# A hybrid encoder in fp32 on one core: one weight block loaded into another buffer, one transposition and some vector steps in new places

## The chip, the cores and the metric

The kernel runs on one core of one Trainium2 chip. The metric is the device time of one execution in microseconds (us). Engines by the names of the profile: PE is TensorE, with PEld its weight loads; DVE is VectorE, ACT ScalarE, POOL GpSimd, and SP the queue of SyncE, which only issues transfers here.

## What is computed

Two layers over 512 tokens of width 1024. Each layer has a mixer (window attention beside a spatial gate) and an MLP of width 4096. The change touches only the start of the MLP and its weights, so the mixer stands here as one line.

```python
for l in range(DEPTH):
    x = x + mixer(rms_norm(x, norm_mix[l]))             # attention beside spatial gating
    h = rms_norm(x, norm_ffn[l])
    x = x + jnp.square(jax.nn.relu(h @ w_up[l])) @ w_down[l]
return rms_norm(x, norm_final)
```

## The kernel before

**Precision by parts.** Every weight block (128x1024, 512 KB) comes into a slot of `raw` (6 slots). ACT rounds it into `whi` (line 932, the high part), and DVE (line 1289; in the mixer and for the first four blocks of an MLP, POOL, line 535) writes what is left into `wlo`, the low part. Both have 5 slots and are used in the order of PE's groups. The other operand is split in the same way (`xhi`/`xlo`, `sxhi`/`sxlo`, `fhi`/`flo`). A product is three matmuls: high by low, high by high, low by high (lines 576 to 581).

**Seven products.** The MLP is done in four quarters of its width. In each, UP (h by w_up) and DOWN (the squared hidden values by w_down) are 2x2 block products by a scheme with seven block products M1 to M7 in place of eight; some factors are sums of blocks. UP runs M1, M2, M7, M6, M4, M5, M3, DOWN runs M1, M7, M6, M4, M5, M2, M3. Each product has two groups of weights (g = 0, 1). An up product is 48 matmuls of 256 columns, a down product 24 of 512. In the last quarter of a layer, `last_products` runs M2 and M3 by halves of the tokens: M2, M3, M2, M3, of 12 matmuls each, with the turns of the next norm between them.

**Where weights come from.** M1 (B11), M2 (B21), M3 and M7 (B22) are plain loads by SP (`load_block`). The weights of M7, M5 and M4 of DOWN are completed by a transfer that POOL issues and that adds a block onto the slot (`add_block`, line 548); those of M6, and M4 of UP, are summed on DVE (`sum_m6` line 1566, `sum_m4` line 1573). `PRODUCT_SLOT` says which pair of slots of `raw` a product has: M7, M6 and M4 share slots 2 and 3 one after another, M1 and M5 slots 0 and 1, M2 and M3 slots 4 and 5. A load waits until the low part of the slot's last block is made (`wait_low`). SP issues in the order of its program and stands at each wait.

**What PE waits for in DOWN.** M6, M4, M5 and M3 build on banks that DVE has just added to the residual `xt` (`add_product`, line 1586): M3 waits for the add of M5, M5 for the add of M6 (`ADDS_TO`). In DVE's order the add of M5 stands behind both low parts of M3.

**Start of the MLP.** The last of the four tiles of the norm is transposed on PE (`turn`, line 603) behind up product M1. From it `xs_make` and `xs_low` (lines 1503 to 1518) build four summed factors: S3 (for M7), S2 (M6), S5 (M5) and S4 (M3); ACT rounds them in `xs_high` (line 1137). `copy_sum` (line 1145) copies M1's, M7's and M6's banks, `up_sum` (line 1529) adds products to them, `hidden` (lines 1157, 1159) makes relu and square. Up product M4 may start when M7's banks are copied, M3 when M5 is summed. The order on each engine is that of its program; no scheduler moves anything.

Of the kernel before, what the change touches and what calls it, by code (L numbers as in the profile page):

```python
# [73 lines left out]
PRODUCT_SLOT = (0, 4, 4, 2, 0, 2, 2)  # L74
# [3 lines left out]
PHASE_LOADS = (1, 1, 1, 1, 2, 2)  # L78
# [29 lines left out]
def loads(l, slot):  # L108
    return l * (MIX_LOADS[slot] + 2 * QUARTERS * PHASE_LOADS[slot])
# [6 lines left out]
def block_loads(l, q, ph, r, g):  # L116

    slot = PRODUCT_SLOT[r] + g
    return loads(l, slot) + MIX_LOADS[slot] + (2 * q + ph) * PHASE_LOADS[slot] + (2 if r == M3 else 1)
# [9 lines left out]
def raw_slot(n):  # L129
    l, pos = divmod(n, PER_LAYER)  # L130
    if pos < MLP_POS:
        return mix_slot(pos)
    i, at = divmod(pos - MLP_POS, PER_PHASE)
    return PRODUCT_SLOT[SEQUENCE[i % 2][at // 2]] + at % 2

# [95 lines left out]
def build(nc, x, gains, weights, sinks, ws, bs, alibi, ident_in, out):  # L231
    with ExitStack() as ctx:
# [206 lines left out]
        def _(sp):  # L439
# [3 lines left out]
            def load_mix(l, pos):  # L443
                if pos >= 4:
                    wait_low(sp, nth(l, pos - 4))
                elif l:
                    wait_low(sp, nth(l - 1, group_pos(QUARTERS - 1, DOWN, M4 if pos < 2 else M5, pos % 2)))
                load(l * LAYER_ROWS + pos, mix_slot(pos))

            def load_block(l, q, ph, r, g):  # L450

                before = divmod(phase(l, q, ph) - 1 - l * 2 * QUARTERS, 2)
                if r == M3:
                    wait_low(sp, nth(l, group_pos(q, ph, M2, g)))
                    if ph == UP:
                        sp.wait_ge(weights_summed, summed_weights(l, q, UP, M4, g))
                elif q or ph:
                    wait_low(sp, nth(l, group_pos(*before, {M1: M5, M7: M4, M2: M3}[r], g)))
                elif r != M2:
                    wait_low(sp, nth(l, MLP_POS - 4 + PRODUCT_SLOT[r] + g))  # L460
                elif l:
                    wait_low(sp, nth(l - 1, group_pos(QUARTERS - 1, DOWN, M3, g)))
                load(block_row(l, q, ph, PRODUCT_BLOCK[r], g), PRODUCT_SLOT[r] + g)
# [33 lines left out]
            for l in range(DEPTH):  # L497
# [31 lines left out]
        def _(pool):  # L529
# [8 lines left out]
            def add_block(l, q, ph, r, g):  # L538

                slot = PRODUCT_SLOT[r] + g  # L540
# [29 lines left out]
        def _(pe):  # L570
# [167 lines left out]
            def up_product(l, q, r):  # L738
# [4 lines left out]
                for m in range(PAIRS):  # L743
                    h, part = divmod(m, 2)
# [90 lines left out]
            for l in range(DEPTH):  # L835
# [78 lines left out]
        def _(act):  # L914
# [66 lines left out]
            for l in range(DEPTH):  # L981
# [199 lines left out]
                xs_high(0)  # L1181
                xs_high(1)
                for q in range(QUARTERS):
                    if q:
# [12 lines left out]
                    hi_up(q, M4, 1)  # L1197
# [23 lines left out]
                    factor_high(q, M4)  # L1221
                    hi_down(q, M4, 0)
                    factor_high(q, M5)
                    hi_down(q, M4, 1)
                    hi_down(q, M5, 0)
                    factor_high(q, M2)
                    hi_down(q, M5, 1)
                    hi_down(q, M2, 0)
                    factor_high(q, M3)
                    hi_down(q, M2, 1)  # L1230
# [30 lines left out]
        def _(dve):  # L1261
# [42 lines left out]
            for l in range(DEPTH):  # L1304
# [256 lines left out]
                def sum_m6(q, ph, g):  # L1561

                    wait_low(dve, nth(l, group_pos(q, ph, M7, g)))
                    dve.wait_ge(raw_landed[PRODUCT_SLOT[M1] + g], 16 * block_loads(l, q, ph, M1, g))
                    t3 = raw_at(PRODUCT_SLOT[M7] + g)
                    dve.tensor_tensor(t3, t3, raw_at(PRODUCT_SLOT[M1] + g), ALU.add).then_inc(weights_summed, 1)  # L1566

                def sum_m4(q, g):

                    wait_low(dve, nth(l, group_pos(q, UP, M6, g)))  # L1570
                    dve.wait_ge(raw_landed[PRODUCT_SLOT[M2] + g], 16 * block_loads(l, q, UP, M2, g))
                    t2 = raw_at(PRODUCT_SLOT[M4] + g)
                    dve.tensor_tensor(t2, t2, raw_at(PRODUCT_SLOT[M2] + g), ALU.add).then_inc(weights_summed, 1)
# [19 lines left out]
                xs_make(0)  # L1593
                xs_make(1)
                xs_make(2)
                xs_low(0)
                xs_make(3)
                xs_low(1)
                for q in range(QUARTERS):
                    low_up(q, M7, 0)  # L1600
                    if q:
                        add_both(q - 1, M3)
                    sum_m6(q, UP, 0)
                    low_up(q, M7, 1)
                    sum_m6(q, UP, 1)
                    if q == 0:
                        xs_low(2)
                    low_up(q, M6, 0)
                    sum_m4(q, 0)
                    low_up(q, M6, 1)  # L1610
                    sum_m4(q, 1)
                    up_sum(q, M2, 0)
                    if q == 0:
                        xs_low(3)
# [144 lines left out]
```

## Time and profile before

| | us |
|---|---|
| three runs | 994.9, 997.0, 997.3 (median 997.0) |
| profiled execution | 992.7, span of the instructions 990.8 |
| PE busy | 943.6 (95%) |
| DVE busy | 707.6 (71%) |
| ACT busy | 562.7 (57%) |
| POOL busy | 204.8 (21%) |
| mean granted clock of TensorE | 0.982 |

A clock of 1.0 is the full 2.4 GHz, 0.5 is 1.2 GHz. Busy times of PE include what its matmuls take at the lower clock. An idle time in the lists has behind it the engine and line that ended it; "issue" means that the profile shows nothing that it waited for.

### The profile page before, as it was taken

How to read it: one execution, taken by the hardware profiler on the slowest of the kernel's cores; microseconds unless marked ns; L12 is line 12 of the kernel's file. 1: busy time of each engine (PE TensorE's matmuls, PEld its weight loads, DVE VectorE, ACT ScalarE, POOL GpSimd, SP SyncE). 2: the span in 40 equal slices, each digit the busy share in tenths (PEclk: the TensorE clock that was granted, in tenths of full speed). 3: DMA queues.
4: the chain of work that ended last, by engine and by line, in shares of the span. 5: the costliest groups of instructions: out<-in, count | busy, mean ns of one | idle time of the engine just before them, and what ended most of it. 6: DMA issues, size and time to landing. Idle time of an engine off the chain costs nothing.

```text
span 990.8 us, 14055 instructions
## 1 busy us (share of the span) xinstructions
PE 943.6 (95%) x5632; PEld 828.1 (84%) x5632; DVE 707.6 (71%) x813; ACT 562.7 (57%) x843; POOL 204.8 (21%) x136
## 2 busy tenths in 40 slices
PE   8999998998999999999799999988989989998995
PEld 5888787987997998898688888888879879988984
DVE  5676436888787878868647761487876977878785
ACT  5556427674665574476455661657546735745753
POOL 2554223110110011001147424401101101100110
PEclk9999999999999999999899999989989999999998
DMA  8432050776577568474534213236838565775653
GB/s 292 136 103 84 22 170 1 192 153 208 140 170 204 133 177 204 121 215 85 190 102 160 78 62 83 87 85 173 193 105 236 122 192 135 168 207 128 173 105 128
DMA packets 40497, 141.76 MB, mean 143 GB/s; under 512 B 5616, under 2 KB 5744, under 8 KB 40432
## 3 DMA queue, kind: packets, MB, share of 16 engines
q1 hardware_dynamic: 28624, 98.32, 29.2%
q0 software_dynamic: 11520, 41.95, 23.9%
q8 instruction: 45, 0.74, 0.3%
q10 hardware_dynamic: 288, 0.59, 0.2%
q14 instruction: 20, 0.16, 0.1%
HBM read 138.74 MB, written 2.10 MB: 142 GB/s over the span
## 4 chain that ended last, share of the span: by engine, by line
PE 57%; DVE 19%; DMA 13%; ACT 5%; issue 5%; POOL 1%; SPq 0%; DVEq 0%; POOLq 0%; ACTq 0%
DMA raw<-weights_in 12%; PE bank L579 10%; PE bank L581 10%; PE bank L580 10%; DVE wlo L1289 9%; PE bank L576 7%; PE bank L578 7%; PE bank L577 7%; DVE flo L1553 3%; ACT whi L932 2%; DVE xt L1586 2%; DVE raw L1566 2%; PE bank L603 1%; PE bank L777 1%; DMA xt<-x_in 1%
## 5 line engine op out<-in xcount | busy, mean ns | idle before, releaser
L932 ACT ACTIVATE whi<-raw 128x1024 fp32r<-128x1024 f32 x268 | 279.5, 1056 | 174.4 <-DMA raw<-weights_in 88.5
L1289 DVE TENSOR_TENSOR wlo<-raw,whi 128x1024 fp32r<-128x1024 f32 x218 | 264.0, 1222 | 108.8 <-ACT whi L932 108.6
L579 PE MATMUL bank<-xhi,wlo 128*128 128x256 f32 (+1 forms) x672 | 211.2, 314 | 11.4 <-issue 8.9
L581 PE MATMUL bank<-xlo,whi 128*128 128x256 f32 (+1 forms) x672 | 209.2, 311 | 0.0
L580 PE MATMUL bank<-xhi,whi 128*128 128x256 f32 (+1 forms) x672 | 209.0, 311 | 0.0
L576 PE MATMUL bank<-wlo,fhi 128*128 128x512 f32 x448 | 179.2, 400 | 23.6 <-DVE xt L1586 20.1
L548 POOL DMA_DIRECT2D raw<-weights_in x80 | 69.4, 868 | 539.6 <-DVE raw L1566 333.1
L577 PE MATMUL bank<-whi,fhi 128*128 128x512 f32 x448 | 177.6, 396 | 0.0
L578 PE MATMUL bank<-whi,flo 128*128 128x512 f32 x448 | 177.5, 396 | 0.0
L535 POOL TENSOR_TENSOR wlo<-raw,whi 128x1024 fp32r<-128x1024 f32 x50 | 135.2, 2716 | 203.4 <-ACT whi L932 203.4
L579 PEld LDWEIGHTS bank<-xhi,wlo 128*128 128x128 f32 x672 | 130.4, 194 | 19.0 <-issue 12.5
L581 PEld LDWEIGHTS bank<-xlo,whi 128*128 128x128 f32 x672 | 130.2, 194 | 6.4
L580 PEld LDWEIGHTS bank<-xhi,whi 128*128 128x128 f32 x672 | 130.4, 194 | 6.1
L576 PEld LDWEIGHTS bank<-wlo,fhi 128*128 128x128 f32 x448 | 86.1, 192 | 45.5 <-issue 27.6
L579 PE MATMUL bank<-sxhi,wlo 128*128 128x256 f32 x384 | 109.6, 285 | 2.5 <-DVE z L1529 2.5
L580 PE MATMUL bank<-sxhi,whi 128*128 128x256 f32 x384 | 109.4, 285 | 0.0
L581 PE MATMUL bank<-sxlo,whi 128*128 128x256 f32 x384 | 109.3, 285 | 0.0
L578 PEld LDWEIGHTS bank<-whi,flo 128*128 128x128 f32 x448 | 86.0, 192 | 18.4
L577 PEld LDWEIGHTS bank<-whi,fhi 128*128 128x128 f32 x448 | 86.3, 193 | 17.5
L579 PEld LDWEIGHTS bank<-sxhi,wlo 128*128 128x128 f32 x384 | 74.4, 194 | 3.0 <-issue 2.9
L581 PEld LDWEIGHTS bank<-sxlo,whi 128*128 128x128 f32 x384 | 74.5, 194 | 0.0
L580 PEld LDWEIGHTS bank<-sxhi,whi 128*128 128x128 f32 x384 | 74.4, 194 | 0.0
(131 smaller groups left out, 1240.7 us busy)
## 6 DMA issues: line engine op xcount, KB each, us to landing
raw<-weights_in SPq DMA_DIRECT2D x172, 512.0 KB, 4.5
raw<-weights_in POOLq DMA_DIRECT2D x80, 512.0 KB, 6.2
xt<-x_in SPq DMA_DIRECT2D x4, 512.0 KB, 8.2
gbc<-gains_in SPq DMA_DIRECT2D x4, 512.0 KB, 4.5
out_t<-xt SPq DMA_DIRECT2D x3, 512.0 KB, 2.7
gbc<-gains_in ACTq DMA_DIRECT2D x1, 512.0 KB, 5.8
bias<-alibi_in SPq DMA_DIRECT2D x2, 256.0 KB, 7.3
wst<-ws_in SPq DMA_DIRECT2D x2, 256.0 KB, 6.9
```

The lines of the kernel that those rows point to most:

```text
L535: pool.tensor_tensor(wlo[:, n % SLOTS, :], raw_at(raw_slot(n)), whi[:, n % SLOTS, :], ALU.subtract) \
L548: pool.dma_start(raw_at(slot), weights[block_row(l, q, ph, B21 if r == M4 else B12, g)], accum_op=ALU.add) \
L576: pe.matmul(o, hi[:, tokens], wlo[:, s, wc], start=first, stop=False, skip_group_check=on_sum)
L577: pe.matmul(o, hi[:, tokens], whi[:, s, wc], start=False, stop=False, skip_group_check=on_sum)
L578: return pe.matmul(o, lo[:, tokens], whi[:, s, wc], start=False, stop=last, skip_group_check=on_sum)
L579: pe.matmul(o, wlo[:, s, wc], hi[:, tokens], start=first, stop=False, skip_group_check=on_sum)
L580: pe.matmul(o, whi[:, s, wc], hi[:, tokens], start=False, stop=False, skip_group_check=on_sum)
L581: return pe.matmul(o, whi[:, s, wc], lo[:, tokens], start=False, stop=last, skip_group_check=on_sum)
L932: act.activation(whi[:, n % SLOTS, :], raw_at(slot), ACT.Copy).then_inc(whi_ready, 1)
L1289: dve.tensor_tensor(wlo[:, n % SLOTS, :], raw_at(raw_slot(n)), whi[:, n % SLOTS, :], ALU.subtract) \
L1553: dve.tensor_tensor(flo[:, f, :, :], src, fhi[:, f, :, :], ALU.subtract).then_inc(hid_lo, 1)
L1566: dve.tensor_tensor(t3, t3, raw_at(PRODUCT_SLOT[M1] + g), ALU.add).then_inc(weights_summed, 1)
```

## The change

Four things change; the work of every engine stays the same in kind and number.

1. In DOWN, M3's block B22 is loaded into slots 2 and 3, behind M4, and no longer into slots 4 and 5 behind M2. So UP M7's load of the next quarter, for the same slots, waits for M3's low parts, and UP M2's, for slots 4 and 5, for those of DOWN M2. SP issues them in the order M3, M1, M2, M7. The first two loads of the next layer wait for M3's low parts too.
2. The last turn stands before the last quarter of M1's matmuls instead of behind them.
3. In the first quarter of a layer, DVE and ACT do the factors' steps in another order.
4. In all quarters some low parts, factors and adds of DOWN M4 to M3 change places.

```diff
-PRODUCT_SLOT = (0, 4, 4, 2, 0, 2, 2)
+PRODUCT_SLOT = ((0, 4, 4, 2, 0, 2, 2), (0, 4, 2, 2, 0, 2, 2))
...
             def load_block(l, q, ph, r, g):
...
                 if r == M3:
-                    wait_low(sp, nth(l, group_pos(q, ph, M2, g)))
+                    wait_low(sp, nth(l, group_pos(q, ph, M2 if ph == UP else M4, g)))
                     if ph == UP:
                         sp.wait_ge(weights_summed, summed_weights(l, q, UP, M4, g))
-                elif q or ph:
-                    wait_low(sp, nth(l, group_pos(*before, {M1: M5, M7: M4, M2: M3}[r], g)))
+                elif ph == DOWN:
+                    wait_low(sp, nth(l, group_pos(q, UP, {M1: M5, M7: M4, M2: M3}[r], g)))
+                elif q:
+                    wait_low(sp, nth(l, group_pos(q - 1, DOWN, {M1: M5, M7: M3, M2: M2}[r], g)))
...
                     for r in (M7, M1, M2):
                         load_blocks(l, q, DOWN, r)
+                    load_blocks(l, q, DOWN, M3)
+                    load_blocks(l, q + 1, UP, M1)
+                    load_blocks(l, q + 1, UP, M2)
                     load_blocks(l, q + 1, UP, M7)
-                    load_blocks(l, q + 1, UP, M1)
-                    load_blocks(l, q, DOWN, M3)
-                    load_blocks(l, q + 1, UP, M2)
...
+                def turn_last(m):
+                    if m == PAIRS - 1:
+                        turn(2 * l + 1, NT - 1)
...
-                        up_product(l, q, r)
-                        if q == 0 and r == M1:
-                            turn(2 * l + 1, NT - 1)
+                        up_product(l, q, r, turn_last if q == 0 and r == M1 else None)
```

ACT's order in the first quarter, up to M7's copy (of the other quarters nothing moves there):

```diff
-                xs_high(0)
-                xs_high(1)
-                    copy_sum(q, M1, 0)
-                    hi_up(q, M7, 1)
-                    copy_sum(q, M1, 1)
-                    if q == 0:
-                        xs_high(2)
-                        xs_high(3)
-                    hi_up(q, M6, 0)
-                    hi_up(q, M6, 1)
-                    hidden(q, M2, 0)
-                    hi_up(q, M4, 0)
-                    hidden(q, M2, 1)
-                    hi_up(q, M4, 1)
+                        xs_high(0)
+                        hi_up(q, M7, 1)
+                        copy_sum(q, M1, 0)
+                        copy_sum(q, M1, 1)
+                        hi_up(q, M6, 0)
+                        xs_high(1)
+                        hi_up(q, M6, 1)
+                        xs_high(2)
+                        hidden(q, M2, 0)
+                        hi_up(q, M4, 0)
+                        xs_high(3)
+                        hidden(q, M2, 1)
+                        hi_up(q, M4, 1)
```

DVE at the start of the MLP of the first layer, before; the first row is the low part of the last turned tile. Lines 1503 to 1512 are `xs_make`, 1518 `xs_low`, 1289 a weight's low part, 1566 and 1573 sums of weights.

```order
L1283 TENSOR_TENSOR xlo<-bank3,xhi 128x4x128
L1503 TENSOR_TENSOR s3<-xf 128x1024
L1506 TENSOR_TENSOR xf<-xf 128x1024
L1509 SCALAR_TENSOR_TENSOR xf<-xf 128x1024
L1518 TENSOR_TENSOR xlo<-s3,xhi 128x4x256
L1512 SCALAR_TENSOR_TENSOR xf<-xf 128x1024
L1518 TENSOR_TENSOR sxlo<-xf,sxhi 128x1024
L1289 TENSOR_TENSOR wlo<-raw,whi 128x1024
L1566 TENSOR_TENSOR raw<-raw 128x1024
```

And in the changed kernel, where the same lines are 1298, 1518 to 1527, 1533, 1304, 1581 and 1588:

```order
L1298 TENSOR_TENSOR xlo<-bank3,xhi 128x4x128
L1518 TENSOR_TENSOR s3<-xf 128x1024
L1304 TENSOR_TENSOR wlo<-raw,whi 128x1024
L1533 TENSOR_TENSOR xlo<-s3,xhi 128x4x256
L1581 TENSOR_TENSOR raw<-raw 128x1024
L1304 TENSOR_TENSOR wlo<-raw,whi 128x1024
L1521 TENSOR_TENSOR xf<-xf 128x1024
L1524 SCALAR_TENSOR_TENSOR xf<-xf 128x1024
L1304 TENSOR_TENSOR wlo<-raw,whi 128x1024
L1533 TENSOR_TENSOR sxlo<-xf,sxhi 128x1024
```

M7's first low part moves from seventh behind the tile to second, the second and third `xs_make` behind both low parts of M7, and the fourth (line 1527) behind the two sums of M2.

DVE in DOWN of the first quarter, before, from the low part of M4's first block. Line 1586 is an add to `xt` (banks 6, 7: M7; 2, 3: M6), 1553 the low part of a factor, 1546 the fourth `make`, which M3's factor is made from.

```order
L1289 TENSOR_TENSOR wlo<-raw,whi 128x1024
L1586 TENSOR_TENSOR xt<-xt,bank6 128x512
L1586 TENSOR_TENSOR xt<-xt,bank7 128x512
L1553 TENSOR_TENSOR flo<-a21,fhi 128x1024
L1289 TENSOR_TENSOR wlo<-raw,whi 128x1024 x2
L1553 TENSOR_TENSOR flo<-hid,fhi 128x1024
L1289 TENSOR_TENSOR wlo<-raw,whi 128x1024
L1586 TENSOR_TENSOR xt<-xt,bank2 128x512
L1586 TENSOR_TENSOR xt<-xt,bank3 128x512
L1289 TENSOR_TENSOR wlo<-raw,whi 128x1024
L1546 SCALAR_TENSOR_TENSOR hid<-hid 128x1024
L1553 TENSOR_TENSOR flo<-hid,fhi 128x1024
```

And in the changed kernel, one row earlier so that the moved factor is seen (lines 1304, 1601, 1568 and 1561):

```order
L1568 TENSOR_TENSOR flo<-a21,fhi 128x1024
L1304 TENSOR_TENSOR wlo<-raw,whi 128x1024
L1601 TENSOR_TENSOR xt<-xt,bank6 128x512
L1601 TENSOR_TENSOR xt<-xt,bank7 128x512
L1304 TENSOR_TENSOR wlo<-raw,whi 128x1024
L1568 TENSOR_TENSOR flo<-hid,fhi 128x1024
L1304 TENSOR_TENSOR wlo<-raw,whi 128x1024
L1601 TENSOR_TENSOR xt<-xt,bank2 128x512
L1601 TENSOR_TENSOR xt<-xt,bank3 128x512
L1304 TENSOR_TENSOR wlo<-raw,whi 128x1024 x2
L1561 SCALAR_TENSOR_TENSOR hid<-hid 128x1024
L1304 TENSOR_TENSOR wlo<-raw,whi 128x1024
```

M5's factor moves ahead of M4's first low part, M2's factor ahead of M5's first low part, M6's adds ahead of M5's second, and M3's factor behind M2's second.

## Rows read from the trace of the kernel before

**Rows 1.** Page, parts 1 and 2: PE's busy time, and the granted clock in tenths.

```profile
PE 943.6 (95%) x5632; PEld 828.1 (84%) x5632; DVE 707.6 (71%) x813; ACT 562.7 (57%) x843; POOL 204.8 (21%) x136
...
PEclk9999999999999999999899999989989999999998
```

**Rows 2.** PE's waits: line, what ended them, us in total, times, longest.

```profile
PE bank L576 <- DVE xt L1586: 20.1, 9, 4.4
PE bank L579 <- issue: 8.9, 2, 4.4
PE bank L576 <- issue: 3.6, 1, 3.6
```

**Rows 3.** Timeline of PE: start, length, instruction, idle before it (M3, M5, M3).

```profile
322.58 0.47 PE L576 MATMUL bank<-wlo,fhi 128*128 128x512 f32 x1 [1.50 <-DVE xt L1586]
...
471.56 0.47 PE L576 MATMUL bank<-wlo,fhi 128*128 128x512 f32 x1 [0.82 <-DVE xt L1586]
...
484.43 0.77 PE L576 MATMUL bank<-wlo,fhi 128*128 128x512 f32 x1 [4.44 <-DVE xt L1586]
```

**Rows 4.** Chain that ended last, around the M3 wait at 322 us: start, length.

```profile
310.67 7.62 DMA raw<-weights_in
...
318.31 1.07 ACT whi L932
...
321.75 0.69 DVE xt L1586
```

**Rows 5.** Stretches of PE: length, busy time (instructions), clock, DMA share, GB/s.

```profile
322.58:401.25 78.67, 78.67 (x504) 1.00 0.68 173
727.17:808.56 81.39, 81.39 (x504) 0.96 0.65 167
811.44:891.71 80.27, 80.27 (x504) 0.98 0.67 168
484.43:498.17 13.74, 13.74 (x61) 0.78 0.62 204
974.08:984.10 10.02, 10.02 (x36) 0.83 0.31 122
683.85:691.33 7.48, 7.48 (x49) 0.77 0.22 89
187.85:200.25 12.40, 11.75 (x97) 1.00 0.95 254
```

**Rows 6.** Timeline of DVE from M4's first low part, second and last quarter.

```profile
300.21 1.23 DVE L1289 TENSOR_TENSOR wlo<-raw,whi 128x1024 fp32r<-128x1024 f32 x1 [1.62 <-ACT whi L932]
301.35 1.28 DVE L1586 TENSOR_TENSOR xt<-xt,bank 128x512 f32<-128x512 f32 x2
...
312.89 1.23 DVE L1553 TENSOR_TENSOR flo<-hid,fhi 128x1024 fp32r<-128x1024 f32 x1 [1.12 <-ACT fhi L1173]
...
462.72 1.23 DVE L1289 TENSOR_TENSOR wlo<-raw,whi 128x1024 fp32r<-128x1024 f32 x1 [3.05 <-ACT whi L932]
```

**Rows 7.** Timeline of PE in the first UP of a layer: M7, M4, M3.

```profile
172.75 0.36 PE L579 MATMUL bank<-xhi,wlo 128*128 128x256 f32 x1 [4.44 <-issue]
...
187.85 0.35 PE L579 MATMUL bank<-xhi,wlo 128*128 128x256 f32 x1 [1.88 <-ACT xf L1145]
...
683.85 0.36 PE L579 MATMUL bank<-sxhi,wlo 128*128 128x256 f32 x1 [1.86 <-DVE z L1529]
```

**Rows 8.** Timeline there: ACT's copy of the turned tile, DVE's sum, M7's copy.

```profile
162.16 1.08 ACT L958 COPY xf<-bank 128x512 f32<-128x512 f32 x2 [2.73 <-PE bank L603]
...
183.88 0.68 DVE L1529 TENSOR_TENSOR z<-first_sum,bank 128x512 f32<-128x512 f32 x1
...
187.14 1.06 ACT L1145 COPY xf<-bank 128x512 f32<-128x512 f32 x2
```

**Rows 9.** Landing times: SP's plain loads 308 to 323, POOL's accumulating 285 to 335.

```profile
DMA to landing us min/median/max: 3.8/4.5/7.6
...
DMA to landing us min/median/max: 5.4/6.4/8.7
```

More of the change, by code:

```diff
@@ L73 @@
 B11, B12, B21, B22 = range(4)
[L74 removed]
+PRODUCT_SLOT = ((0, 4, 4, 2, 0, 2, 2), (0, 4, 2, 2, 0, 2, 2))
 PRODUCT_BLOCK = {M1: B11, M2: B21, M3: B22, M7: B22}
 MIX_LOADS = (5, 5, 6, 6, 0, 0)
[L78 removed]
+QUARTER_LOADS = (2, 2, 3, 3, 3, 3)
+LOADED_AS = ({M1: 1, M2: 1, M3: 2, M7: 1}, {M1: 2, M2: 3, M3: 3, M7: 2})
 PHASE_ROWS = KC
@@ L108, in loads @@
 def loads(l, slot):
-    return l * (MIX_LOADS[slot] + 2 * QUARTERS * PHASE_LOADS[slot])
+    return l * (MIX_LOADS[slot] + QUARTERS * QUARTER_LOADS[slot])
 def mix_slot(pos):
@@ L116, in block_loads @@
 def block_loads(l, q, ph, r, g):
-    slot = PRODUCT_SLOT[r] + g
-    return loads(l, slot) + MIX_LOADS[slot] + (2 * q + ph) * PHASE_LOADS[slot] + (2 if r == M3 else 1)
+    slot = PRODUCT_SLOT[ph][r] + g
+    return loads(l, slot) + MIX_LOADS[slot] + q * QUARTER_LOADS[slot] + LOADED_AS[ph][r]
 def block_adds(l, q, ph, r):
@@ L538, in add_block @@
             def add_block(l, q, ph, r, g):
-                slot = PRODUCT_SLOT[r] + g
+                slot = PRODUCT_SLOT[ph][r] + g
                 if r == M7:
@@ L743, in up_product @@
                 for m in range(PAIRS):
+                    if before_chunk is not None:
+                        before_chunk(m)
                     h, part = divmod(m, 2)
@@ L1179, in hi_down @@
                     hi(group_pos(q, DOWN, r, g))
-                xs_high(0)
-                xs_high(1)
                 for q in range(QUARTERS):
-                    if q:
-                        hi_up(q, M7, 0)
-                    copy_sum(q, M1, 0)
-                    hi_up(q, M7, 1)
-                    copy_sum(q, M1, 1)
-                    if q == 0:
-                        xs_high(2)
-                        xs_high(3)
-                    hi_up(q, M6, 0)
-                    hi_up(q, M6, 1)
-                    hidden(q, M2, 0)
-                    hi_up(q, M4, 0)
-                    hidden(q, M2, 1)
-                    hi_up(q, M4, 1)
+                    if q == 0:
+                        xs_high(0)
[11 more added lines that the diff above has]
+                        hi_up(q, M4, 1)
+                    else:
+                        hi_up(q, M7, 0)
+                        copy_sum(q, M1, 0)
+                        hi_up(q, M7, 1)
+                        copy_sum(q, M1, 1)
+                        hi_up(q, M6, 0)
+                        hi_up(q, M6, 1)
+                        hidden(q, M2, 0)
+                        hi_up(q, M4, 0)
+                        hidden(q, M2, 1)
+                        hi_up(q, M4, 1)
                     copy_sum(q, M7, 0)
@@ L1591, in add_both @@
                     add_product(q, r, 1)
[L1593 to L1598, printed above, removed]
-                for q in range(QUARTERS):
-                    low_up(q, M7, 0)
-                    if q:
-                        add_both(q - 1, M3)
[L1603 to L1614, printed above, removed]
-                    up_sum(q, M2, 1)
+                for q in range(QUARTERS):
+                    if q == 0:
+                        xs_make(0)
+                        low_up(q, M7, 0)
+                        xs_low(0)
+                        sum_m6(q, UP, 0)
+                        low_up(q, M7, 1)
+                        xs_make(1)
+                        xs_make(2)
+                        low_up(q, M6, 0)
+                        xs_low(1)
+                        sum_m6(q, UP, 1)
+                        low_up(q, M6, 1)
+                        sum_m4(q, 0)
+                        up_sum(q, M2, 0)
+                        sum_m4(q, 1)
+                        up_sum(q, M2, 1)
+                        xs_make(3)
+                        xs_low(2)
+                        xs_low(3)
+                    else:
+                        low_up(q, M7, 0)
+                        add_both(q - 1, M3)
+                        sum_m6(q, UP, 0)
+                        low_up(q, M7, 1)
+                        sum_m6(q, UP, 1)
+                        low_up(q, M6, 0)
+                        sum_m4(q, 0)
+                        low_up(q, M6, 1)
+                        sum_m4(q, 1)
+                        up_sum(q, M2, 0)
+                        up_sum(q, M2, 1)
                     low_up(q, M4, 0)
```

39 lines of the change are left out of this document (19 added, 20 removed).

## The prediction

> **What bounds the kernel now.** I read the page first: PE is busy 95% of 990.8 us, and the granted clock is full in all but a few slices [rows 1]. So PE is the bound, and the gain can only come from its idle time and from stretches at half clock. The list of waits says where PE idles: 20.1 us in nine waits on `xt<-bank` of VectorE (line 1586, the adds of the down products), one of 3.6 us at the same kind of place put down to "issue", and 8.9 us in two waits before an up product [rows 2]. The timeline of PE puts the first kind at one place: seven of the nine waits and the 3.6 us one stand before product M3 of DOWN, one in each of the 2 x 4 quarters (18.8 + 3.6 us); the other two, 0.4 and 0.8 us, stand before M5. Two of the M3 waits and one M5 wait stand as samples in [rows 3]. The 8.9 us are 4.44 us twice, before up product M7 of the first quarter of a layer.
>
> Why M3 waits is read from the chain of work that ended last, in the quarter at 300 us: the low part of M2's second block ends, a load of 512 KB is issued behind it and takes 7.62 us, ScalarE rounds it at 318.31, VectorE makes its low part and only then, in its own order, adds M5 at 321.75, for which M3's banks wait until 322.58 [rows 3, 4]. The load is B22 for M3; it waited for M2's slot. So a buffer is what is late, not the engine behind it.
>
> The waits cost twice. A full-clock quarter takes 78.67 us from M3 to M3; in the second layer one takes 81.39 (2.72 more) and one 80.27 (1.60 more), at a mean clock of 0.96 and 0.98 and with no PE idle in between; the 13.74 us behind the 4.44 us wait ran at 0.78 (3.0 us lost), the last 10.02 us at 0.83 (1.7 us lost) [rows 5]. The half-clock stretches stand right at the longer waits, so with the waits they should go. Sum 9.0 us.
>
> **B22 in M4's place.** No instruction is added; 16 loads (2 in each quarter) now wait for M4's low parts. M4's first low part starts at 300.21 and ends at 301.4, the second would end near 304, so the loads are issued at 301.5 and 304.2 in place of 310.67 and 315.3. With the 7.62 us of the slow one they land by 312. What is late next is VectorE's own order. From M4's first low part (300.21) to the first add of M5 it now has eleven 1024-wide steps at a pitch of 1.14 us (eight low parts, two factors' low parts, `make`: 12.5), six 512-wide adds at 0.6 (3.6), that add itself (0.7) and 0.4 of waiting for ScalarE's second high part [rows 6]. The 1.12 us wait for M3's `fhi` behind `make` is now covered by M2's second low part, which moves ahead of it. 17.2 us: the add ends near 317.4. PE, not held, wants M3 at 322.58 - 1.50 = 321.08 [rows 3]. Spare: 3.7 us. The wait goes whole in the six quarters that are not the last of a layer. In the last quarters the products M2 and M3 run by halves, and M3 is wanted 2.9 us earlier. Layer 0: M4's low part 462.72 [rows 6] + 17.2 = 479.9, while PE, without the 0.82 us before M5, arrives at 484.43 - 4.44 - 0.82 = 479.2 [rows 3]: 0.7 us stay, and about 0.4 us at the turn behind it, which needs a norm built on the same add. Layer 1: PE does not wait, but the tail runs on VectorE's and ScalarE's norms behind the same add, which moves by 4.2 us, not by the 3.6 + 1.7 of PE: 1.1 us stay. The waits before M5 go, since the adds of M6 move ahead of a low part and M5's factor is made while VectorE waits anyway (1.62 us at 300.21, [rows 6]). Sum: 20.1 + 3.6 + 9.0 - 1.1 - 1.1 = 30.5 us.
>
> What is queued behind the moved waits: on SP, UP M7's load for the next quarter falls back from 301.46 to 315.7, since M3 now holds its slot, and GpSimd's accumulating transfer falls with it. Worked out for the quarter at 300 us: the load lands after 4.5 (median) to 7.6 us, the accumulation after 0.9 us of issue and 6.4 to 8.7 us, high and low part take 2.3 us [rows 4, 9]. That is ready at 329.8 to 335.2; PE wants it two up products (11.9 us) behind the end of M3 at 326.7, at 338.6. A cover of 3.4 us or more, so I cost it at nothing; at its high end in every quarter it would still be nothing. ScalarE sits behind it for up to 3 us, before a copy that PE needs only at M6. Layer 1's first weights now wait for M3's low part, at 477.9, about when they were issued before; the norm they must beat is ready at 482.8: nothing.
>
> **The start of UP in the first quarter.** The last turn comes 12 matmuls earlier in M1 (97 in 11.75 us: 0.121 each [rows 5]), 1.44 us. Its data are copied at 160.7 in place of 162.16 [rows 8]. VectorE then makes s3, M7's low part, s3's low part: ready at 166.5, before PE ends M2 at 172.75 - 4.44 = 168.31 [rows 7]. The 4.44 us go. But M7 and M6 (11.8 us) now end at 180.1, and M4 needs M7's copy, which ScalarE makes only behind both halves of M2's hidden values and M4's high parts. Before: second sum of M2 on VectorE 183.88, copy 187.14, PE 187.85 [rows 7, 8]. After: 1.44 us from the turn, three steps fewer ahead of the sums (a `make` and two low parts, 3.5 us), 0.2 us from neighbours that no longer hang on one another (pitch 1.14 for 1.25), less a wait of 1.1 us for M6's second high part: that sum at 179.8; then ScalarE must wait for the fourth `make` (181.6) before it rounds it, and the copy comes at 184.7, 2.4 us earlier than 187.14. So PE waits there 185.4 - 180.1 = **5.3 us at one place**, where it waited 4.44 + 1.88 us at two. Before, the loss of clock behind the 4.44 us wait cost nothing, since M4 waited anyway (1.88 us idle [rows 7]). Now it falls on M4 and M5, which have only 0.65 us of cover: the 4.44 us waits were followed by 3.4 to 6.1 us of half clock, so 1.7 to 3.1 us. Layer 0: M3 starts at 185.4 + 11.85 + 1.7 to 3.1 = 199.0 to 200.4, before 200.25; gain 1.3 to -0.1 us, I take 0.6. Layer 1: the same at 667.8, M3 at 681.3 to 682.8, before 683.85, and the half clock behind that wait (0.77 over 7.48 us, 1.7 us lost [rows 5, 7]) goes: gain 2.7 to 4.3, I take 3.2. Together 3.8 us.
>
> The Trainium skill (TensorE: Matmul & The Clock Gate, What's actually happening) says that half rate is the gate's default state and that activity releases it. By that rule the new 5.3 us wait ends at half clock. The trace bears it out for both 4.44 us waits and not for every short one: the 1.88 us wait at 187.85 was followed by 12.40 us at 1.00, the 1.86 us one at 683.85 by 0.77. If the clock stayed full behind the new wait, the time would be about 4 us less.
>
> **Sum.** 992.7 (the profiled execution) - 30.5 - 3.8 = 958.4 us. The three runs have a median of 997.0, 4.3 above the profiled one; part of that may be the same waits and clock, so I carry 3 us: **961.5 us**.
>
> **Rivals.**
> - *VectorE takes the place of the load* (0.13): its 17.2 us are packed by hand; 5 us more (late landings, ScalarE behind UP M7) leave about 1.5 us at eight places and a third of the clock loss: 961.5 + 12 + 3 = 976.
> - *The first quarter gives back* (0.15): its slack is thin (M6's second half is ready within 0.2 us of need, and the load of DOWN M1 lands just before it is used). Two more waits of 1.5 us and their clock in each layer: 968. Against it: the chain ahead of UP M3 moves by the same 2.4 us as PE.
> - *Slower: UP M7 late* (0.03). Load and accumulation stand one behind the other, 12 to 17 us in all behind M3's low part. PE waits once the pair takes 20.6 us, at six places (three quarters of each layer); the gain of 34 us is eaten when each wait exceeds 5.7 us, so from 26 us for the pair. With 7 us each: 961.5 + 42 = 1003. Against: the longest of each kind in these windows sum to 17 us [rows 9].
> - *The load does not move* (0.04): SP issues in order, and M3's loads stand behind M2's, whose wait may be the true one. Then only the adds and the first quarter gain: 988. Against: M2's loads wait for UP M3's low parts, long done. Within this case half lies near no change (0.02).
>
> **How the numbers follow.** Forecast 0.65, rivals as given. The range reaches from the forecast with full clock behind the new waits, and nothing carried (954), to past the first two rivals (979). 0.3% is about what a measurement of this kernel can tell from no change. Faster 0.94, same 0.03, slower 0.03.
>
> **What would show it.** Right: no PE idle over 0.3 us before DOWN M3 in six quarters and under 1 us in the last ones; PE's waits on the adds fall from 20.1 to under 2 us; B22's loads issued about 10 us earlier; the clock row full from 200 us to the layer's end; one wait near 5 us before UP M4 in each layer, none before UP M7. Wrong: PE waits on `wlo` or `whi` before UP M7, or M3 still released by the add of M5 with VectorE never idle ahead of it.

## The result, and the profile after

The changed kernel takes **959.4 us** (median of 4 runs, 958.02 to 960.21). The kernel before took 995.9 us in the same comparison (993.02 to 997.27). The ratio is 0.9636 with a 95% interval of 0.9609 to 0.9662: 3.6% faster. The profiled execution took 959.93 us, with a span of 958.1 us and a mean clock of 0.990; before it was 992.7, 990.8 and 0.982.

The page of the changed kernel, parts 1 and 2, against [rows 1]:

```profile
PE 932.8 (97%) x5632; PEld 822.5 (86%) x5632; DVE 707.3 (74%) x813; ACT 562.4 (59%) x843; POOL 204.9 (21%) x136
...
PEclk9999999999999999999999999998999999999999
```

Every engine executes as many instructions as before. PE's busy time is 10.8 us less because less of it runs at half clock, and the row shows one slice below 9, where [rows 1] shows four.

PE's waits in the changed kernel, against [rows 2] (line, what ended them, us in total, times, longest):

```profile
PE bank L581 <- ACT xf L1151: 10.5, 2, 5.2
PE bank L581 <- DVE z L1544: 4.7, 3, 2.5
PE bank L833 <- DVE pp L1307: 2.0, 1, 2.0
```

No wait on an add of the down products is left: the 20.1 and 3.6 us of [rows 2] are gone. The 8.9 us of the two 4.44 us waits are gone too. In their place 10.5 us stand in two waits on line 1151, the copy of M7's banks before UP M4, and 4.7 us in three waits on an `up_sum`, two before UP M3 and one in the middle of it (0.72 us in layer 1). On the same two steps PE had waited before as well, 2.6 and 2.5 us (lines 1145 and 1529), so the first quarters' waits are 14.0 us before and 15.2 after. The new ones, of both layers, on PE's timeline (start, length, instruction, idle before it), against [rows 7]:

```profile
185.64 0.55 PE L581 MATMUL bank<-xhi,wlo 128*128 128x256 f32 x1 [5.25 <-ACT xf L1151]
...
201.26 0.36 PE L581 MATMUL bank<-sxhi,wlo 128*128 128x256 f32 x1 [2.47 <-DVE z L1544]
...
654.26 0.55 PE L581 MATMUL bank<-xhi,wlo 128*128 128x256 f32 x1 [5.25 <-ACT xf L1151]
...
670.02 0.36 PE L581 MATMUL bank<-sxhi,wlo 128*128 128x256 f32 x1 [1.53 <-DVE z L1544]
```

Where the time went is read from the moments at which PE starts the same stage in both kernels. Each row gives how much earlier the changed kernel starts it, in us; a rise from row to row is what the stretch between them gained.

| start of | layer 0 | layer 1 |
|---|---|---|
| UP M1, quarter 0 | -0.2 | 13.6 |
| UP M7, quarter 0 | 4.4 | 18.2 |
| UP M4, quarter 0 | 2.2 | 16.0 |
| UP M3, quarter 0 | -1.0 | 13.8 |
| DOWN, quarter 0 | -2.3 | 14.4 |
| quarter 1 | 1.3 | 20.2 |
| quarter 2 | 3.0 | 25.0 |
| quarter 3 | 5.0 | 28.1 |
| next layer, or last matmul | 13.6 | 33.5 |

From UP M1 to M7 the new start gains 4.6 us in each layer, and by the start of DOWN most or all of it is given back: UP of the first quarter comes out at -2.2 us in layer 0 and +0.8 us in layer 1, together -1.4 us. DOWN and what follows it bring 34.3 us. The other -0.2 us stand ahead of UP. At the end of the execution the gain is 32.7 us (990.8 - 958.1), 0.8 us less than at the last matmul.

### The profile page after: what moved, and what is told of

Same layout as the page of the kernel before. It is cut to its first block, busy times and chain, and to the rows that moved or that the text cites. A ratio compares the mean times of both kernels' runs of the same rounds, so it can differ in the third digit from the quotient of the medians.

```text
span 958.1 us, 14055 instructions
## 1 busy us (share of the span) xinstructions
PE 932.8 (97%) x5632; PEld 822.5 (86%) x5632; DVE 707.3 (74%) x813; ACT 562.4 (59%) x843; POOL 204.9 (21%) x136
## 4 chain that ended last, share of the span: by engine, by line
PE 85%; DVE 6%; DMA 3%; ACT 3%; issue 2%; POOL 0%; DVEq 0%; ACTq 0%; POOLq 0%
PE bank L578 14%; PE bank L580 14%; PE bank L579 14%; PE bank L581 13%; PE bank L583 13%; PE bank L582 13%; DMA raw<-weights_in 3%; DVE wlo L1304 2%; PE bank L605 1%; PE bank L833 1%; PE bank L781 1%; DVE raw L1581 1%; PE bank L816 1%; PE bank L826 1%; PE bank L807 1%
## 5 line engine op out<-in xcount | busy, mean ns | idle before, releaser
L581 PE MATMUL bank<-xhi,wlo 128*128 128x256 f32 (+1 forms) x672 | 211.0, 314 | 10.5 <-ACT xf L1151 10.5
L578 PE MATMUL bank<-wlo,fhi 128*128 128x512 f32 x448 | 174.7, 390 | 0.0
L579 PE MATMUL bank<-whi,fhi 128*128 128x512 f32 x448 | 174.4, 389 | 0.0
L580 PE MATMUL bank<-whi,flo 128*128 128x512 f32 x448 | 174.3, 389 | 0.0
L578 PEld LDWEIGHTS bank<-wlo,fhi 128*128 128x128 f32 x448 | 84.1, 188 | 17.6 <-DVE flo L1568 0.4
L579 PEld LDWEIGHTS bank<-whi,fhi 128*128 128x128 f32 x448 | 84.1, 188 | 17.2
```

Source lines behind the costliest of these rows:

```text
L578: pe.matmul(o, hi[:, tokens], wlo[:, s, wc], start=first, stop=False, skip_group_check=on_sum)
L579: pe.matmul(o, hi[:, tokens], whi[:, s, wc], start=False, stop=False, skip_group_check=on_sum)
L580: return pe.matmul(o, lo[:, tokens], whi[:, s, wc], start=False, stop=last, skip_group_check=on_sum)
L581: pe.matmul(o, wlo[:, s, wc], hi[:, tokens], start=first, stop=False, skip_group_check=on_sum)
```

## Experiments

**The two parts apart.** Four kernels ran on one chip, against the same runs of the kernel before. The first keeps all but the new start of UP: the last turn stands behind M1 again, with the old order of the factors' steps.

```diff
-                        up_product(l, q, r, turn_last if q == 0 and r == M1 else None)
+                        up_product(l, q, r)
+                        if q == 0 and r == M1:
+                            turn(2 * l + 1, NT - 1)
```

> The changed kernel with the start of UP in the first quarter put back as it was (turn behind M1, the old order of VectorE and ScalarE there); slots, loads and the order in DOWN as changed. Against 995.9 us before and 959.4 changed. By the profile of the changed kernel the new start loses 2.3 us in layer 0 (PE at DOWN of the first quarter 208.58 for 206.25) and keeps 0.8 in layer 1: then this kernel takes about 958 us (957 to 959). By the prediction, which gave the new start 3.8 us, it takes 963.

Measured: 961.3 us (959.03 to 963.46), ratio 0.965 (0.9593 to 0.9707), between the two values expected. The old start costs 1.9 us against the changed kernel by the medians; the ranges of the two overlap, and they ran in different comparisons, so this is not told from zero. Its waits (same columns) have the old 8.9 us back:

```profile
PE bank L581 <- issue: 8.9, 2, 4.4
PE bank L581 <- DVE z L1537: 4.1, 3, 2.5
PE bank L581 <- ACT xf L1153: 3.1, 2, 1.9
```

These 16.1 us of waits in the first quarters compare with 15.2 in the changed kernel. One wait stayed in DOWN (line 1594, left out above), 1.75 us before M3 in the last quarter of layer 0; in the changed kernel it is absent.

The second keeps, of the whole change, the slots and the order of the loads only; the old order of VectorE's and ScalarE's steps in DOWN is back as well.

> Only the slots of B22 and the order of the loads are changed; VectorE's and ScalarE's orders and the turn are those of before. If the buffer was the cause, nearly all of the gain is here: VectorE's old order needs 19.6 us from M4's low part to the add of M5 in place of 17.2, still in time in six quarters, 2.4 us late in the two last ones: 958 + 5 + 1.2 (M5's waits) and some half clock, 964 to 967 us. If the order is what matters and the load was only a companion, it stays above 980.

Measured: 967.38 us (966.69 to 970.21), ratio 0.9717 (0.966 to 0.9773), 0.4 us above the range expected. Of the 23.7 us of waits in DOWN 2.8 are left:

```profile
PE bank L578 <- issue: 2.1, 2, 1.3
PE bank L578 <- DVE xt L1594: 0.7, 2, 0.4
```

The first two stand before M3 in the last quarters of the layers, the others before M5. So the slot is what M3's waits hung on.

The third is the kernel before with the new start of UP alone.

> The kernel before with only the new start of UP in the first quarter (turn inside M1 and the new orders there). By the prediction 992 us (3.8 gained). By the profile of the changed kernel, in which the loads of DOWN M1 take 9 to 11 us there, 995 to 998: no gain, perhaps a small loss.

Measured: 996.23 us (989.06 to 1003.07, 10 runs) against 996.79 for the kernel before, ratio 1.000 (0.9958 to 1.0043). Its waits show the trade by itself: 10.5 us before M4 and 5.1 at M3 of UP for the 8.9, 2.6 and 2.5 us before, and 23.1 us in DOWN for the 23.7 of [rows 2]:

```profile
PE bank L576 <- DVE xt L1599: 15.3, 7, 3.2
PE bank L579 <- ACT xf L1149: 10.5, 2, 5.2
PE bank L576 <- issue: 7.8, 2, 4.1
PE bank L579 <- DVE z L1542: 5.1, 3, 2.8
```

The fourth is the kernel before with the new order of VectorE's and ScalarE's steps in DOWN alone.

> The kernel before with only the new order of VectorE's and ScalarE's steps in DOWN; B22 still waits for M2's slot. M2's low parts come 0.8 and 3 us earlier, so its two loads start that much earlier: each M3 wait of 1.5 to 4.4 us shrinks by 0.8 to 1.5 us, M5's 1.2 us go, a part of the 9 us of half clock with them: 982 to 988 us. If the order alone frees M3 (rival), 965 or less; if only the slot counts, 995.

Measured: 980.5 us (978.1 to 983.48), ratio 0.9845 (0.9784 to 0.9905), 1.5 us under the range expected. Its waits in DOWN are shorter and not gone, 15.4 us for 23.7:

```profile
PE bank L576 <- DVE xt L1586: 12.8, 6, 3.2
PE bank L579 <- issue: 8.9, 2, 4.4
PE bank L576 <- issue: 2.6, 2, 1.5
```

The 8.3 us of waits are only half of the gain. The waits before M3 in the first three quarters of layer 1 are as long as before (3.13, 3.21 and 2.73 us for 3.15, 2.88 and 2.83), but PE runs at full clock behind them, where [rows 5] shows 0.96 and 0.98 (length, busy time, clock, DMA share, GB/s):

```profile
719.14:801.05 81.91, 78.70 (x505) 1.00 0.67 167
801.05:882.45 81.40, 78.67 (x505) 1.00 0.67 169
```

Why waits of the same length cost clock in one kernel and none in the other is open, and how much of the 16.3 us is owed to the order itself is open with it.

So the slots alone take 29.4 us off, the order alone 16.3, and both (`b_only`) 35.5. They don't add up: both shorten the same path to the add of M5, and with the slots alone only 2.8 us of waits are left for the order to take. The new start of UP is worth nothing that these runs can tell from zero. Their intervals reach 4 to 6 us to either side, so by the medians alone the 3.8 us forecast are not ruled out; the stages of the trace above are what speaks against them.

**Where the start of UP gives its gain back.** In the changed kernel PE waits twice there: 5.25 us for M7's copy, which ScalarE makes behind M4's high parts, and then up to 2.5 us for the sum of M5. What holds that sum in layer 0 is read from two timelines. VectorE's, against the 200.25 us at which PE started M3 before:

```profile
199.29 1.22 DVE L1304 TENSOR_TENSOR wlo<-raw,whi 128x1024 fp32r<-128x1024 f32 x1 [4.96 <-ACT whi L938]
```

And ScalarE's, which makes the high part of the same block just before:

```profile
198.21 1.06 ACT L938 ACTIVATE whi<-raw 128x1024 fp32r<-128x1024 f32 x1 [3.13 <-DMA raw<-weights_in]
```

VectorE stands idle for 4.96 us in front of a low part of DOWN M1, whose load has not landed; the sum of M5 is queued behind it. ScalarE had waited for the transfer. The two issues of DOWN M1's loads of layer 0 in the kernel before, from issue to landing:

```profile
DMA to landing us min/median/max: 5.5/6.5/7.5
```

And in the changed kernel:

```profile
DMA to landing us min/median/max: 8.8/10.2/11.5
```

The first of them is issued 2.2 us earlier than before (189.35 for 191.56) and lands 1.1 us later (198.18 for 197.09). In layer 1 the two took 6.8 and 9.2 us before and 9.0 and 11.6 after.

Four kernels followed, again on one chip, each in five rounds. The first is the changed kernel itself, unaltered, as the measure for the others.

> The changed kernel itself, as the reference on this chip for the three others: 959.4 us as before (958 to 961), with waits of 5.25 us before UP M4 in both layers and 1.5 to 2.5 us before UP M3.

Measured: 960.01 us (958.74 to 962.47), before 999.42, ratio 0.9625 (0.9581 to 0.9669).

The second moves each of M5's sums ahead of one of DOWN M1's low parts, in every quarter, so that the first sum no longer waits for a load and the second only for the first load (VectorE shown; on ScalarE M4's second and M5's first hidden values move ahead of M1's high parts in the same way):

```diff
-                    low_down(q, M1, 0)
                     up_sum(q, M5, 0)
-                    low_down(q, M1, 1)
+                    low_down(q, M1, 0)
                     up_sum(q, M5, 1)
+                    low_down(q, M1, 1)
```

> The changed kernel with M5's sums and M4's hidden values moved ahead of DOWN M1's high and low parts, so that nothing on the way to UP M3 waits for DOWN M1's load. If that load, 9 to 11 us from issue to landing where 6.6 were forecast, is the cause of the 2.5, 1.5 and 0.7 us waits at UP M3, they go, with the half clock behind the one in layer 0 (1.7 us): 954 to 956 us. If VectorE's chain as a whole is late (rival), the wait only moves to DOWN M1 or M7 and the time stays within 1 us of the changed kernel's.

Measured: 959.3 us (957.21 to 962.32), ratio 0.9616. The waits before UP M3 are gone, so M1's load is what held it. But no gain shows in the median, where 954 to 956 us were expected; the rival named there, that the wait only moves on, is nearer. The waits:

```profile
PE bank L581 <- ACT xf L1151: 10.5, 2, 5.2
PE bank L833 <- DVE pp L1307: 2.0, 1, 2.0
PE bank L578 <- DVE flo L1568: 1.7, 2, 1.2
```

A part of the time comes back as 0.5 and 1.2 us before DOWN M6, whose factor is now late. The profiled execution is 2.8 us shorter than that of `after_again` (957.44 for 960.23), but it is one of the two fastest of six; why the median doesn't follow was not found.

The third makes M7's copy and M4's low parts in the first quarter earlier, so that M4 can start (ScalarE shown).

```diff
                         xs_high(2)
+                        copy_sum(q, M7, 0)
+                        copy_sum(q, M7, 1)
                         hidden(q, M2, 0)
                         hi_up(q, M4, 0)
-                        xs_high(3)
                         hidden(q, M2, 1)
                         hi_up(q, M4, 1)
+                        xs_high(3)
```

> The changed kernel with the copy of M7's banks moved ahead of M2's hidden values and M4's low parts ahead of the fourth make and the last two factors' low parts, in the first quarter. The wait of 5.25 us before UP M4 then falls to 2 to 2.5 us in both layers (copy at 178 for 184.9, M4's first low part at 182.5). If UP M3 is held by DOWN M1's load, as the trace has it, PE arrives there earlier and waits longer, and only 0 to 2 us are gained: 957 to 959. If not, 6 us are gained: 953.

Measured: 958.03 us (957.54 to 960.24), ratio 0.9606, as expected. The 5.25 us wait is 2.18 us. M3 is held all the same, by the same load; the two rows are from PE's timeline:

```profile
182.45 0.35 PE L581 MATMUL bank<-xhi,wlo 128*128 128x256 f32 x1 [2.18 <-issue]
...
198.04 0.55 PE L581 MATMUL bank<-sxhi,wlo 128*128 128x256 f32 x1 [2.79 <-DVE z L1547]
```

The fourth does both.

> Both edits. PE reaches UP M3 about 5 us earlier in layer 0 and is held by nothing there; then VectorE is late for DOWN M7's factor, by about 2 us. So 3.5 to 4.5 us for each layer: 950 to 953 us. If the rival holds (VectorE's chain as a whole sets the end of the first quarter), no better than the better one of the two.

Measured: **955.46 us** (954.9 to 957.1), ratio 0.958 (0.9541 to 0.962). It is 4.5 us below the changed kernel on the same chip, and the two sets of runs don't overlap. Each edit alone gave 0.7 and 2.0 us. Together they stay short of the 950 to 953 us expected. The waits left in the first quarters:

```profile
PE bank L581 <- issue: 6.0, 4, 2.2
PE bank L578 <- DVE flo L1571: 4.7, 2, 2.9
PE bank L581 <- DVE z L1547: 1.1, 3, 0.7
```

They have moved on once more: 4.7 of 11.8 us stand before DOWN M6, whose factor waits for what was moved in front of it. The 1.1 us are the second half of UP M3 for the most part, whose sum still stands behind M1's first low part.

**Why the load is slow.** The next four ran on one chip. The first is the changed kernel with one more wait on SP: M2's loads of DOWN are issued only when the low part of the same block of M1 is made. In layer 0 the first of them then starts at 200.26 in place of 192.03, and M1's second load lands at 201.65, so they hardly run beside M1's.

```diff
+                    if r == M2:
+                        wait_low(sp, nth(l, group_pos(q, DOWN, M1, g)))
```

> The changed kernel with the two loads of DOWN M2 in every quarter held until the low part of the same block of DOWN M1 is made. In the first quarter they then no longer share the engines with DOWN M1's loads, which took 8.8 and 11.5 us from issue to landing (5.5 and 7.5 before the change). If the crowd of transfers is the cause of that, M1's loads land in 6 to 8 us and the waits before UP M3 (2.44 us in layer 0, 1.74 + 0.70 in layer 1) fall to 1.5 us or less in each layer: 956.5 to 958.5 us. If the loads are slow for another reason (their neighbours are GpSimd's accumulating transfers), they stay at 8 us or more and the time at 959 to 961.

Measured: 958.63 us (958.01 to 959.29), ratio 0.9618. M1's loads took 8.6 and 11.3 us in layer 0, against 8.8 and 11.5 in the changed kernel, so M2's loads are not what slows them. The median is under the 959 to 961 us expected for this case, but inside the spread of the changed kernel's runs.

**The price of a late UP M7.** In the changed kernel UP M7's load is issued later. Three rows, of one quarter, show how; in none of the six quarters does PE wait there. SP's issue of the load for the quarter at 325 us:

```profile
314.35 0.33 SPq L442 DMA_DIRECT2D raw<-weights_in  x1
```

The issue of the accumulating transfer, on POOL's timeline, once the load has landed:

```profile
318.01 0.86 POOL L550 DMA_DIRECT2D raw<-weights_in  x1 [22.99 <-DMA raw<-weights_in]
```

ScalarE's step on the block, and what ended its idle time:

```profile
325.37 1.06 ACT L938 ACTIVATE whi<-raw 128x1024 fp32r<-128x1024 f32 x1 [1.66 <-PE bank L580]
```

The load lands in about 3.7 us, the accumulation in 5.8, and ScalarE's step is released by PE and not by the transfer. To see what a slow pair would do, the accumulation was held back until the first half of UP M1 was done, some 10 us:

```diff
+                    if q and ph == UP:
+                        pool.wait_ge(w_used, nth(l, group_pos(q, UP, M1, 0)) + 1)
```

> The changed kernel with GpSimd's accumulating transfers of UP M7, in the six quarters that are not a layer's first, held until PE is done with the first half of UP M1: about 10 us later than now (318.0 to 328.2 in the quarter at 325 us). If only the arrival at UP M7 counted, as the prediction had it, the cover there takes it all up: 960 to 962 us. If the sums and copies queued behind M7's parts on VectorE and ScalarE are what PE meets next (UP M4 waits for M7's copy, some 5.6 us of cover against 8.6 us of delay), about 3 us at each of six places: 976 to 985 us. Above 997 only if each place costs over 6 us.

Measured: 1001.81 us (998.49 to 1009.2, 10 runs), ratio 1.0064 (1.0033 to 1.0094), 0.6% slower than the kernel before and well above the 976 to 985 us expected. Its waits (line, what ended them, total, times, longest; the two of 5.25 us in the first quarters are among them as in the changed kernel):

```profile
PE bank L583 <- ACT xf L1153: 26.8, 8, 5.2
PE bank L583 <- DVE z L1546: 15.4, 13, 3.3
```

One of those before UP M4, on PE's timeline:

```profile
273.22 0.36 PE L583 MATMUL bank<-xhi,wlo 128*128 128x256 f32 x1 [2.71 <-ACT xf L1153]
```

PE hardly waits at M7 itself (0.3 us). It waits before M4 and M3, since ScalarE and VectorE stood for 10 us in front of M7's parts with M7's copy and the sums queued behind. Each of the six quarters lost 6.4 to 9.0 us: 2.7 us of idle before M4, 1.9 on average at M3, 0.3 at M7, 1.7 us for the 3.4 us at half clock that each of the six had, and the rest in what a wait costs beyond its idle time (0.25 us each, see below).

**What is left before DOWN M6.** The last two are `both_free` with one more edit each. This one puts M1's adds and M6's factor ahead of the second low part of M6:

```diff
-                    low_down(q, M6, 1)
                     add_both(q, M1)
                     factor_low(q, M6)
+                    low_down(q, M6, 1)
```

> The kernel with both edits (955.5 us), and in every quarter the adds of M1 and M6's factor on VectorE ahead of M6's second low part. PE's waits before DOWN M6 (1.76 us in layer 0, 2.93 in layer 1, ended by that factor) shrink by one low part, 1.14 us, in each layer, and the half clock behind the second one may go: 952 to 954.5 us. If the wait moves to M6's second half or to DOWN M4, whose accumulation waits for that low part, 955 to 956.

Measured: 959.77 us (958.02 to 961.91), ratio 0.963, where 955 to 956 us was the worst expected. The waits before M6 are gone and DOWN M3 waits again in both last quarters; one of them:

```profile
474.08 0.47 PE L578 MATMUL bank<-wlo,fhi 128*128 128x512 f32 x1 [1.72 <-DVE xt L1604]
```

By the program M4's accumulation, and with it all behind it, hangs on the low part that the edit made late; that this is what held M3 was not tried by itself. Another part has nothing to do with the edit. The second half of UP M3 waited 1.87 us in layer 0 and 3.24 us in layer 1 (0.71 us and less in `both_free`), and in layer 0 all that stands ahead of it is the same in both kernels: M1's loads took 8.2 and 9.3 us in this execution and 7.0 and 8.3 in that one.

The other adds the late loads of M2:

> The kernel with both edits and the late loads of DOWN M2. If the crowd of transfers holds DOWN M1's loads, VectorE gets M1's low parts about 1.5 us earlier and everything behind them in the chain to DOWN M6 with it: 952.5 to 954.5 us. If not, 955 to 956 as without it.

Measured: 957.98 us (956.41 to 959.43), ratio 0.9609, with 2.5 us before M6 in both layers. M1's loads took 6.6 and 8.6 us and in `both_free` 7.0 and 8.3: no difference to explain. These two ran in another comparison than `both_free`, so the 4.3 and 2.5 us by which they are longer are less sure than the waits themselves.

## Why the prediction was right, and where it was not

The forecast was 961.5 us, the median is 959.4: faster, and 2.1 us from it. The sum against the profiled execution was 958.4, and 959.93 was measured. The two parts of that sum missed in opposite directions, by 3.8 us too little in DOWN and 5.2 us too much in UP. That the total came so close is in part luck, since the two misses nearly cancel; that the slot brings most of the gain, and how, was worked out.

**B22 in M4's place: forecast 30.5 us, measured 34.3.** The mechanism is the one told. SP issues B22's loads at 300.17 and 302.80, where the prediction had 301.5 and 304.2 and before it was 310.67; these rows are SP's:

```profile
300.17 0.33 SPq L442 DMA_DIRECT2D raw<-weights_in  x1
302.80 0.33 SPq L442 DMA_DIRECT2D raw<-weights_in  x1
```

VectorE's own order is then what ends last. The timeline of VectorE, against [rows 6], from M4's first low part to the add of M5, with the `make` and the last of M3's low parts between them:

```profile
298.91 1.23 DVE L1304 TENSOR_TENSOR wlo<-raw,whi 128x1024 fp32r<-128x1024 f32 x1 [0.45 <-ACT whi L938]
...
308.43 1.22 DVE L1561 SCALAR_TENSOR_TENSOR hid<-hid 128x1024 f32<-128x1024 f32 x1
...
313.11 2.35 DVE L1304 TENSOR_TENSOR wlo<-raw,whi 128x1024 fp32r<-128x1024 f32 x2
315.38 0.68 DVE L1601 TENSOR_TENSOR xt<-xt,bank 128x512 f32<-128x512 f32 x1
```

The path ends at 316.06, 17.15 us after 298.91; forecast 17.2. PE takes M3 at 319.67, a spare of 3.6 us; forecast 3.7. A chain of eighteen steps was priced within 0.1 us; each had a row at its own pitch. The quarters then run like this (length, busy time, clock, DMA share, GB/s), against [rows 5]:

```profile
246.69:325.11 78.42, 78.42 (x506) 1.00 0.72 178
715.17:793.59 78.42, 78.42 (x505) 1.00 0.70 173
```

PE has no idle time in either and the full clock in both. The 3.8 us over the forecast are two terms. The sum counted each wait at its idle time, but a held quarter loses 0.25 us more: before, M3 starts at 322.58 and 402.92, 80.34 us apart with 1.67 us of idle, and an undisturbed quarter takes 78.42 us from start to start. Over ten waits that is 2.4 us. The other mis-sized term is the 2.2 us that were to stay in the last quarters of the two layers; 0.8 stayed. In layer 1 the tail kept them much as forecast (1.1): the last matmul gains 5.4 us on that quarter, the end of the execution 4.6. In layer 0 nothing stayed (forecast 1.1): M4's first low part came 12.0 us behind the start of DOWN (455.85 for 443.84), and 13.9 us before (462.72 for 448.79, [rows 6]), so the whole path began 1.9 us nearer to PE. The prediction let it start at its old place.

```profile
455.85 1.22 DVE L1304 TENSOR_TENSOR wlo<-raw,whi 128x1024 fp32r<-128x1024 f32 x1 [0.55 <-ACT whi L938]
```

The wait of 3.05 us for a high part that stood before it is 0.55 us. `b_only`, in which 1.75 us were left at this place, shows that it is near the edge.

**The start of UP: forecast 3.8 us, measured -1.4 in the profile, and 0.6 and 1.9 in the medians of `a_only` and `b_only`.** Up to UP M4 every step came out: low part of s3 ready at 166.7 (166.5), second sum of M2 at 180.0 (179.8), the fourth `make` at 181.8 (181.6), M7's copy at 184.9 (184.7), PE's wait 5.25 us (5.3) and its start 185.64 (185.4). The step that failed is the next: "M3 starts at 185.4 + 11.85 + 1.7 to 3.1". It took M4, M5 and the clock as the only things ahead of M3. The chain to M3 also goes through VectorE's queue, where a low part of DOWN M1 stands ahead of the sum of M5, and through the load of that block, which took 8.8 and 11.5 us where such loads took 5.5 and 7.5 before. PE was done with M5 at 198.79, in time, and M3 started at 201.26 and not at 199.0 to 200.4. The rival "the first quarter gives back" named this load as the thin place, at 0.15, and priced the give-back at 6.5 us over both layers; 5.2 us of gain are missing. What was put against it, that the chain ahead of UP M3 moves by the same 2.4 us as PE, held for the issue of the load (2.2 us earlier) and not for its landing (1.1 us later). So this rival took place, with its mechanism and most of its size, while the other term covered it. That this order is what holds M3 is shown by `m3_free`, in which the waits before it go; what they cost in the whole time is less sure, since its median gains only 0.7 us.

**The clock.** The windows of PE from M4 to M3 of the two layers, then M3 of layer 0:

```profile
185.64:201.26 15.62, 13.15 (x96) 0.90 0.89 238
654.26:668.49 14.23, 14.22 (x96) 0.80 0.88 223
201.26:208.92 7.66, 7.66 (x50) 0.78 0.17 65
```

Behind each 5.25 us wait PE ran at half clock for a while, 1.2 GHz for 2.4, as forecast. The Trainium skill (TensorE: Matmul & The Clock Gate, What's actually happening) has half rate as the default that activity releases. By that rule such a wait ends at half clock, and for these two waits the trace agrees. The 4 us that a clock staying full would have given did not come. In layer 0 the lost clock cost nothing in the end, since M3 waited anyway (2.47 us), but that wait had a half-clock stretch behind it too.

**The rivals.** "VectorE takes the place of the load" did not happen; no add of M5 held PE in any of the eight quarters. "The load does not move" did not either. "Slower: UP M7 late" did not happen, since the pair took about 9.5 us in the quarter shown and not 20.6. But its price was mis-sized. The prediction put the point from which PE waits at a pair of 20.6 us, reckoned to M7's own need. `m7_late` put the pair at about 20 us (18.9 and 20.2 in its first case), and PE lost 6.4 to 9.0 us in each quarter, with the kernel slower than before. The step that failed there is the one about ScalarE, "before a copy that PE needs only at M6": the copies and sums queued behind the late part are needed by M4 and M3, and these wait first. Taking PE's 2.71 us before M4 off the 10 us by which the parts were late leaves a cover of some 7 us, so the waits begin at a pair of about 17 us; this is worked out from one point and is an estimate. The chance of 0.03 was low enough for what happened, but the place was nearer than told.

**The sum.** 3 us were carried because the three runs before lay above their profiled one. They were not needed: the median after is 0.5 us below its profiled execution. In one comparison the runs of the kernel before spread from 990.1 to 1004.0 us and those of the changed kernel from 958.7 to 962.5. The spread is smaller with most of the waits gone; what makes it was not tried.

## What to carry to other kernels

When PE waits for a buffer's refill, look whose slot it is: moving 16 loads to a slot that came free some 10 us earlier took away nearly all of the wait, and the half clock behind it was gone too. A wait in front of a step is not only that step's: in queues that run in order, price the slip for everything behind it, and ask which of those steps is needed first. Where an order is written by hand, a moved wait comes back at the next thin place; here three edits in a row met a new one, at M4, M3 and M6, and of the edits to the first quarter only two made together gained more than these runs leave in doubt.

## What the hardware showed that was not expected

- Two plain loads of 512 KB of the same kind took 5.5 and 7.5 us in one order and 8.8 and 11.5 us in another (layer 1: 6.8 and 9.2, 9.0 and 11.6), while 512 KB took 3.7 us elsewhere in the same trace. In that stretch they run beside accumulating transfers, which took 9.3 and 10.8 us there themselves. Holding M2's loads back did not shorten them. What does slow them stays open. `m4_early` and `both_free` start DOWN M7's loads and accumulating transfers some 2 to 3 us earlier and M1's loads at the same time as the changed kernel, and M1's loads of layer 0 took 5.8 and 9.1, 7.0 and 8.3 us, which fits the accumulating transfers as the cause. But `m3_free` moves no transfer there and had 7.1 and 9.8 us, so part of the difference comes and goes between executions, and no run moved those transfers alone.
- A wait of PE has a half-clock stretch behind it in some cases and not in others of the same length. In layer 0 of `both_free` waits of 2.17 and 1.76 us had none, and in its layer 1 a wait of 2.94 us came with 3.4 us of half clock; in the changed kernel 3.4 us of it followed 2.47 us, and in `order_only` waits of 3.13 and 3.21 us had none. So a clock loss could be priced only as a range.
